# Row transfers of an expert stage: the write first, the fetch two units later

## What is computed

```python
E_FF = 7 * D_MODEL // 2          # 3584
N_EXPERTS, TOP_K = 8, 2

def moe_swiglu(h, w_router, b_router, w_gu, w_down):
    logits = (h @ w_router).astype(jnp.float32) + b_router.astype(jnp.float32)
    top_logit, top_idx = lax.top_k(logits, TOP_K)
    top_w = jax.nn.softmax(top_logit, axis=-1)
    gates = jnp.sum(jax.nn.one_hot(top_idx, N_EXPERTS, dtype=jnp.float32) * top_w[..., None], axis=-2)
    ...
    for e in range(N_EXPERTS):
        out = out + gates[..., e:e + 1] * swiglu(h, w_gu[e], w_down[e])
    return out
```

## Time and profile before

| | us |
|---|---|
| median of three runs | 1377.65 |
| the profiled execution, own time | 1374.81 |
| its span (first to last instruction) | 1373.0 |
| TensorE matmuls busy | 1337.8 |
| VectorE, ScalarE, GpSimd busy | 449.9, 318.4, 42.1 |
| the chain that ended last | TensorE 90%, DMA 8% |
| expert stage, by the trace | about 480 to 1313 |

### The profile page before, as it was taken

How to read it: one execution, slowest core, us unless ns; L and a number is a source line. 1 busy time by engine, 2 the same in 40 slices (tenths; PEclk the granted TensorE clock), 3 DMA queues, 4 the chain that set the end, 5 groups by cost and what they waited for, 6 DMA issues and landing times.

```text
span 1373.0 us, 76894 instructions
## 1 busy us (share of the span) xinstructions
PE 1337.8 (97%) x35943; PEld 1165.6 (85%) x35943; DVE 449.9 (33%) x835; ACT 318.4 (23%) x530; POOL 42.1 (3%) x61
## 2 busy tenths in 40 slices
PE   8999999999999789999999999999999999998998
PEld 6888888888888689999988888988998888887876
DVE  7887555557886400200200200200210110021224
ACT  7565444446533300010010010010010010011112
POOL 1010000000000100000000000000000000000000
PEclk9999999999999999999999999999999999999999
DMA  8477555556423889999999999999999999999960
GB/s 317 178 248 248 187 188 191 193 176 242 158 89 136 338 302 412 421 400 422 422 406 421 423 402 422 422 397 417 422 405 422 422 411 405 421 422 419 422 284 31
DMA packets 75679, 448.46 MB, mean 327 GB/s; under 512 B 9580, under 2 KB 9580, under 8 KB 31984
## 3 DMA queue, kind: packets, MB, share of 16 engines
q1 hardware_dynamic: 70848, 435.19, 80.2%
q0 software_dynamic: 4640, 12.58, 2.7%
q10 hardware_dynamic: 144, 0.03, 0.0%
HBM read 442.48 MB, written 7.08 MB: 327 GB/s over the span
## 4 chain that ended last, share of the span: by engine, by line
PE 90%; DMA 8%; issue 1%; DVE 1%; ACT 0%; POOL 0%; SPq 0%; POOLq 0%; DVEq 0%; ACTq 0%
PE PS L984 35%; PE PS L551 10%; PE PS L553 10%; PE PS L552 10%; PE PS L1006 9%; PE PS L1015 7%; DMA raw<-in_e_w_down 5%; PE PS L1010 3%; DMA SC<-in_e_w_gu 2%; DMA SC<-in_e_w_down 1%; PE PS L602 1%; PE PS L846 0%; PE PS L692 0%; PE PS L620 0%; PE PS L956 0%
## 5 line engine op out<-in xcount | busy, mean ns | idle before, releaser
L984 PE MATMUL PS<-gain,raw 128*32 128x88 f32 x14464 | 290.8, 240 | 10.5 <-issue 7.6
L984 PEld LDWEIGHTS PS<-gain,SC 128*32 128x32 f32 x14208 | 285.6, 111 | 9.2 <-issue 2.9
L984 PEld LDWEIGHTS PS<-gain,raw 128*32 128x32 f32 x14464 | 281.7, 111 | 12.4 <-issue 8.3
L984 PE MATMUL PS<-gain,SC 128*32 128x88 f32 x14208 | 285.7, 240 | 3.3 <-issue 2.3
L551 PE MATMUL PS<-w_hi,xT_hi 128*128 128x512 f32 x536 | 212.9, 397 | 0.5 <-DVE w_lo L1519 0.5
L553 PE MATMUL PS<-w_lo,xT_hi 128*128 128x512 f32 x536 | 209.0, 390 | 0.0
L552 PE MATMUL PS<-w_hi,xT_lo 128*128 128x512 f32 x536 | 208.7, 389 | 0.0
L1411 ACT ACTIVATE junk<-PS 128x352 f32<-128x352 f32 x56 | 26.0, 464 | 750.1 <-PE PS L984 750.1
L2028 DVE TENSOR_TENSOR junk<-junk,PS 128x352 f32<-128x352 f32 x56 | 29.2, 521 | 513.8 <-ACT junk L1411 507.1
L1519 DVE TENSOR_TENSOR w_lo<-raw,w_hi 128x1024 fp32r<-128x1024 f32 x144 | 168.9, 1221 | 23.3 <-ACT w_hi L1117 21.6
L1015 PE MATMUL PS<-raw,he 128*32 128x256 f32 x660 | 154.7, 385 | 9.7 <-DMA raw<-in_e_w_down 9.7
(11 more groups left out here) (305 smaller groups left out, 975.3 us busy)
## 6 DMA issues: line engine op xcount, KB each, us to landing
raw<-in_e_w_gu SPq DMA_DIRECT2D x113, 1024.0 KB, 11.4
SC<-in_e_w_gu SPq DMA_DIRECT2D x111, 1024.0 KB, 11.6
SC<-in_e_w_down SPq DMA_DIRECT2D x57, 1024.0 KB, 11.6
raw<-in_e_w_down SPq DMA_DIRECT2D x55, 1024.0 KB, 11.7
raw<-in_ffn_w_gu SPq DMA_DIRECT2D x44, 512.0 KB, 4.7
raw<-in_w_in_c SPq DMA_DIRECT2D x32, 512.0 KB, 5.5
raw<-in_ffn_w_down SPq DMA_DIRECT2D x22, 512.0 KB, 5.0
raw<-in_w_in_ab SPq DMA_DIRECT2D x20, 512.0 KB, 7.1
```

The costliest lines, as they stand in the source:

```text
L984: m = pe.matmul(PS[32 * f:32 * (f + 1), side, b * SLOTS:b * SLOTS + CAP], paired[:, b // 2, b % 2, 32 * f:32 * (f + 1)], xe[:, k, :], star ...
```

## The change

Two things are edited, both on GpSimd. The write of an item's loop turn now stands ahead of the fetch, in the loop and ahead of it. And `fetch_rows(i)` has one more wait: `used` must have reached the count at which TensorE has done the first two turns of the unit loop of item i (2 * 2 * RING above the count at the item's start). Nothing else changes.

```diff
             def fetch_rows(i, first=False):
                 pool.wait_ge(src_ready, i + 1)
+                pool.wait_ge(used, i * (EU * 2 * RING) + (2 * (G_MOE + 4) + 2 * 2 * RING))
                 if first:
...
+            write_rows(0)
             fetch_rows(0, True)
-            write_rows(0)
...
             with pool.Fori(1, last_item) as i:
+                write_rows(i)
                 fetch_rows(i)
-                write_rows(i)
             write_rows(last_item)
```

## The result

The changed kernel took 1380.1 us (median of 17 runs, 1377.03 to 1383.26), the kernel before, beside it, 1377.11 us (17 runs, 1374.82 to 1380.51). The ratio is 1.0021, with a 95% interval of 1.0014 to 1.0028: 2.9 us slower, between 1.9 and 3.9. The forecast was 1.9 us slower. So the sign of the sum was right, and its size lies at the low edge of what was measured. The point value lies just above the 0.2% that were to count as no change, and the 17 runs of each kernel tell apart less than that: the interval is 0.07% wide on either side.

A forecast was written before the change was run, and what follows sets the result against it. The prediction took the DMA engines to bound the expert stage. Write first, later fetches, separation and clock at 0, first fetch +1.9 us: 1377.65 + 1.9 = 1379.5 us for the median, range 1375.2 to 1384.2.

The forecast's parts named there:

- The DMA engines are the bound: Expert stage: it ends when the DMA engines have moved all they are given; loads landing 11.7 us after issue leave no reserve.
- the prediction's price: Expert stage, full weight stream: a fetch costs 2.3 us, 0.62 for its bytes plus 1.69 of lost rate.
- The loss is the fetch's and the write's is small: Row transfers beside the weight stream: the whole 1.69 us loss is the fetch's; a write costs 0.7 us with its bytes.
- Write first, at 0: GpSimd, each item: the write is issued about 1 us earlier, nobody waits for it, bytes and price stay: 0.
- The fetch later, at 0: GpSimd, each item: the fetch waits for two units of TensorE, with 34 us of cover before VectorE's turn: no wait.
- Apart or together, at 0: Items 1 to 6: separate fetch and write cost 3.0 us, the pair 2.9: nothing won or lost; bounds -2.6 to +3.2.
- The second rival: Items' fetches: a fetch alone is dearer than in a pair, 1383.7 us; decides from a loss of 1.88 us; chance 20%.
- the dearest price: Items 1 to 6: each lone fetch loses 2.22 us like the dearest pair, instead of 1.69: +3.2 us together.
- The first fetch, at +1.9 us: Stage start: the first fetch moves from an idle gap into the nearly full stream, costing 1.45 to 2.3 us, taken as 1.9.
- The clock gives nothing back: TensorE's granted clock falls after long waits; separated waits may avoid that, but it gains nothing while DMA sets the end.
- The upper end, 1383.7 + 0.4: Top of the median's range, given as 1384.2 us: dearer lone fetches plus the 0.4 us by which runs lie over their median.
- the forecast's own range: Whole kernel: -1.6 to +3.7 us around the forecast, which was given a chance of 63%.

The follow-up runs named there:

- a fast fetch: The kernel before, with the fetch spread over 128 partitions instead of 88, the 40 added rows out of bounds: 1369.62 us against 1377.81, ratio 0.9945.

## Why the prediction was right in sign and short in size

**The DMA engines are the bound: right.** What was taken from or given to the DMA engines came back in the time, in full or for the greater part: -14.3 us without fetched rows (13.8 by the prediction's price), -7.6 with a fast fetch (10.1 by the rate), -4.6 without written rows (4.9), +2.9 with the first fetch in the stream. Landing times rise in steps and do not fall between them, before and after.

**The loss is the fetch's and the write's is small: right.** The lone fetches, the lone writes and the two kernels that leave one of them out say it independently. The reason given for it, that the dip begins before the write can move and ends with the fetch, was enough.

**Write first, at 0: right in price.** 420 GB/s beside it, and no new wait. The write was to be issued about 1 us earlier, and that was a misreading. ScalarE's last row for the second write in the changed kernel is

```profile
593.01 1.16 ACT L1428 ACTIVATE SC<-PS 32x256 f32<-32x256 f32 x3
```

It ends at 594.17, and the write is issued 0.96 us later, at 595.13. Before, it was 0.95 us (593.30 - 592.35), so nothing shows that the fetch had held the write up.

**The fetch later, at 0: right.** VectorE's turn has kept its place behind the units and waits for no fetch. How long the second fetch took to land (operation, count, median us from issue), and the turn, in the changed kernel:

```profile
SC<-xbuf,seg POOLq DMA_INDIRECT x1, 10.4
```

```profile
668.93 3.11 DVE L2011 STREAM_TRANSPOSE xn<-SC 32x256 f32<-32x256 f32 x7
```

Issued at 623.41, landed at 633.8, turned from 668.9 on: 35 us of cover, where 34 were forecast. (The view of the turn ends at 672, so it counts 7 of the 12 instructions.)

**Apart or together, at 0: right, and closer than its bounds.** 1.69 us each way. The second rival needed 1.88 us per lone fetch; one of the six reaches that, their mean does not. Fetches without written rows came near it, with a mean of 1.87 us. What decides is the time: with the first fetch early and six fetches late and alone the ratio was 0.9994 (0.9982 to 1.0006), at most 0.8 us slower than before, where the dearest price asked for 3.2.

**The first fetch, at +1.9 us: the term that was too small.** The full price of 2.3 us had been cut by half of 0.85 us of room, room read from 398 GB/s between 515 and 530. That mean hides two parts. The fetch was issued at 518.74, and its rows move some 4 us later. In the kernel before, that stretch and the one ahead of it are:

```profile
515.00:520.00 5.00, 5.00 (x242) 4.90 (x237) 0.36 (x1) 0.00 (x0) 0.00 (x0) 1.00 0.99 377
520.00:533.00 13.00, 13.00 (x498) 12.44 (x491) 0.88 (x2) 0.46 (x1) 0.00 (x0) 1.00 1.01 413
```

By the rate, most of the room lay in 515 to 520, where no row of the fetch had yet moved; from 520 it was 13 x (1 - 413/422) = 0.28 us. By the share of time for which the DMA engines were busy there was next to none: 0.99 and 1.01 in these two rows, 1.00 in the earlier trace rows. A low rate beside a share of 1.00 is not idle time, and the prediction took it for room. The parts of the loads say so too: in the kernel before, the mean of a load's 16 steps rises from 5.3 us (issued 506:512) to 6.5 (524:531), so the stream was falling behind there. Why it moves less in that time, no row shows.

Nor was this fetch an average one: it lost 2.06 us of rate. 2.06 + 0.62 = 2.7 us, as much as the 2.7 us by which the landing times stand higher, and inside the measured 1.9 to 3.9. With 0.28 us of room taken off it would be 2.4, inside as well; the runs don't decide between the two. The forecast of 1.9 us lies on the edge of the interval. Of the 0.8 us that it is short of 2.7, half is room that was not there and half the loss above the mean. The upper end that the prediction gave for this term, 2.3, took the mean loss of the pairs and not their dearest; it lies inside the interval too. Nor was the early place wholly free, it seems: in 530:545 loads land after 7.2 us in the kernel before and after 6.8 where no rows are fetched, one execution of each.

**The clock gives nothing back: right.** The granted clock is 1.00 in every stretch of the changed kernel above, where 0.86 and 0.88 stood, that is, it stays at the 2.4 GHz level. TensorE could go faster in those stretches, and the stage still took longer.

**Two figures of the range.** The upper end, 1383.7 + 0.4, comes to 1384.1 and not 1384.2. The +3.7 of the forecast's own range is not worked out in the prediction. Neither touches the forecast.

## What to carry to other kernels

When transfers set the end of a stage, as here, moving a transfer in time is free only between places that are equally full; a gap at the stage's start is worth the transfer's bytes and its disturbance, and a transfer that sits in it should stay there. To see how much room a stretch has, cut it where the moved transfer's packets begin, not where its issue stands, look at the share of time for which the DMA engines are busy and not at the rate alone, and read how the landing time of the main stream steps. And before moving a disturbing transfer, ask why it disturbs: here its shape was worth 8 to 12 us, its place 3.

## What the runs showed of the hardware

Not expected was that a gather of the same 64 or so rows costs the weight stream 1.7, 1.0 or under 0.1 us of rate, by whether it is written for 88, 96 or 128 partitions, and that the scatter in the other direction costs some 0.1 us at 88. Nor that dealing the same rows over both halves of the partitions brought another 3.2 us (1370.01 to 1366.77), which no rate shows and the last part of each load does.

The trace names no DMA engine, so which engine moved which row isn't seen. The Trainium skill ("DMA: Bandwidth & Descriptors", section "The descriptor swizzle") states that in a transfer to 128 partitions each DMA engine writes the partitions of one port of its own, engines 0 to 7 those below 64 and engines 8 to 15 those from 64 on. By that, 64 rows in places 0 to 63 would load only half of the engines, and the spread kernel both halves; its gain agrees, and so do the loads' first and last steps. That a gather is dealt out like such a transfer is inferred. How the rows are dealt out over 88 and 96 partitions no run here shows, and why 96 stands between the two stays open.
